# Expert weights read as one run of 16 or 8 KB per partition, with the tokens permuted to match

## The reference

```
p_group = softmax(h @ w_group);  g = argmax(p_group)
p_exp   = softmax((h @ w_expert) inside group g);  the best 2 experts, weights renormalised, times p_group[g]
for each expert e:   ffn[tokens of e] += weight * ((silu(h @ w_gate[e]) * (h @ w_up[e])) @ w_down[e])
h = layer_norm(ALPHA * h + ffn)
```

## Time and profile before

| | us |
|---|---|
| median of the timed runs | 2484.46 |
| the profiled execution, whole | 2484.86 |
| its span, first to last instruction | 2483.1 |
| TensorE busy | 2119.0 (85%) |
| VectorE busy | 667.5 |
| ScalarE busy | 313.5 |
| GpSimd busy | 175.2 |
| first and last gateup of layer 0 | 333.31 to 823.7 |
| first and last gateup of layer 1 | 1087.85 to 1576.4 |

### The profile page before, as it was taken

The page is one execution under the profiler, slowest core; times in us unless marked ns, Lnnn a source line. Parts: engine busy times, 40 slices in busy tenths (PEclk is TensorE's granted clock), DMA queues, the critical chain, the costliest instruction groups (busy, mean ns, idle before and its releaser), DMA issues. The chain is left out here.

```text
span 2483.1 us, 33384 instructions
## 1 busy us (share of the span) xinstructions
PE 2119.0 (85%) x13513; PEld 1427.3 (57%) x13513; DVE 667.5 (27%) x2009; ACT 313.5 (13%) x841; POOL 175.2 (7%) x224
## 2 busy tenths in 40 slices
PE   8999789888877498679878888488889989889997
PEld 7776466556555344366555555244478734448863
DVE  4354321111111315421111111328432112833211
ACT  2122000000000013100000000012322101222100
POOL 0112101000000100000000000100001100000110
PEclk9999867777888697767777777689899999989999
DMA  9333459999999742259999999852144342212420
GB/s 335 125 129 109 128 210 396 395 394 395 394 392 393 288 159 95 85 208 363 395 395 395 395 395 394 302 201 102 38 145 142 142 169 103 101 68 102 169 85 25
DMA packets 246122, 574.69 MB, mean 231 GB/s; under 512 B 13316, under 2 KB 16634, under 8 KB 245534
## 3 DMA queue, kind: packets, MB, share of 16 engines
q1 hardware_dynamic: 242974, 569.46, 62.0%
q0 software_dynamic: 3072, 4.21, 0.5%
HBM read 568.39 MB, written 9.44 MB: 233 GB/s over the span
## 5 line engine op out<-in xcount | busy, mean ns | idle before, releaser
L981 PE MATMUL ps<-ring,arena 128*32 128x256 f32 x3968 | 301.8, 469 | 107.6 <-DMA ring<-in_moe_w_up_dram 55.9
L981 PEld LDWEIGHTS ps<-ring,arena 128*32 128x32 f32 x3968 | 169.9, 135 | 250.5 <-issue 207.6
L2097 PE MATMUL ps<-arena,ring 128*128 128x256 f32 x1408 | 304.4, 379 | 1.6 <-DVE arena L244 1.6
L2097 PEld LDWEIGHTS ps<-arena,ring 128*128 128x128 f32 x1408 | 267.4, 190 | 38.5 <-DVE arena L244 2.3
L959 PEld LDWEIGHTS ps<-arena,h 128*128 128x128 f32 x2112 | 256.4, 202 | 29.5 <-issue 26.4
L959 PE MATMUL ps<-arena,h 128*128 128x32 f32 x2112 | 264.0, 286 | 3.0 <-DVE arena L949 3.0
L1394 PE MATMUL ps<-ring,arena 128*128 128x512 f32 (+1 forms) x576 | 250.9, 595 | 2.4 <-DVE arena L244 1.6
L1021 PE MATMUL ps<-ring,arena 128*32 128x256 f32 x1984 | 212.0, 602 | 38.1 <-issue 37.0
L266 PE MATMUL ps<-ring,arena 128*128 128x512 f32 x544 | 239.0, 602 | 1.6 <-DVE arena L1434 0.8
L1394 PEld LDWEIGHTS ps<-ring,arena 128*128 128x128 f32 x576 | 110.1, 193 | 136.2 <-issue 132.4
L266 PEld LDWEIGHTS ps<-ring,arena 128*128 128x128 f32 x544 | 104.8, 193 | 133.2 <-issue 130.4
(11 more groups left out here) (295 smaller groups left out, 1781.5 us busy)
## 6 DMA issues: line engine op xcount, KB each, us to landing
ring<-in_moe_w_gate_dram SPq DMA_DIRECT2D x62, 2048.0 KB, 19.4
ring<-in_moe_w_up_dram SPq DMA_DIRECT2D x62, 2048.0 KB, 22.4
ring<-in_moe_w_down_dram SPq DMA_DIRECT2D x62, 2048.0 KB, 19.8
ring<-in_w_up_dram SPq DMA_DIRECT2D x22, 2048.0 KB, 7.8
ring<-in_ssm_w_in_dram SPq DMA_DIRECT2D x12, 2048.0 KB, 12.2
ring<-in_w_in_dram SPq DMA_DIRECT2D x10, 2048.0 KB, 11.7
ring<-in_w_down_dram SPq DMA_DIRECT2D x10, 2048.0 KB, 7.8
ring<-in_attn_w_qkv_dram SPq DMA_DIRECT2D x6, 2048.0 KB, 20.2
```

The source lines that it names most:

```text
L981: mm = nc.tensor.matmul(ps[j * CAP:(j + 1) * CAP, 2 + b, 0:256], xg[:, b, k * CAP:(k + 1) * CAP], w[:, k, (j % 2) * 256:(j % 2 + 1) * 256] ...
L2097: mm = nc.tensor.matmul(ps[:, n % 4, 0:SEQ], w[:, k, k4 * P:(k4 + 1) * P], xT_mlp[:, k, :], start=(k == 0), stop=(k == KD - 1))
```

## The change

Gate and up matrices are read with `"(p k) n -> p k n"`: partition p gets the rows 8p to 8p + 7, which lie behind each other, 16 KB in all. Down matrices are read with `"(a p k) n -> p a k n"`, a = 2: partition p gets the rows 2p and 2p + 1 of each half of the matrix, two runs of 8 KB. Bytes, slots, the order of the loads and their waits stay. To match the new order of the contraction, pick takes its stationary operand from `h_rows`, a copy of h with the columns in the order k, p, that ScalarE makes once per layer in the place of `xT`; TensorE waits for it ahead of the first pick. And turn reads every second column of the hidden values.

```
         def dst(self, c, shape):
+            if len(shape) == 4:
+                return self.rows4(c).rearrange("p (a k) n -> p a k n", a=2)
...
-                add(cols8(t["moe_w_gate"][layer, e], 0, FF))
-                add(cols8(t["moe_w_up"][layer, e], 0, FF))
-                add(rows4(t["moe_w_down"][layer, e], 0))
+                add(t["moe_w_gate"][layer, e].rearrange("(p k) n -> p k n", p=P))
+                add(t["moe_w_up"][layer, e].rearrange("(p k) n -> p k n", p=P))
+                add(t["moe_w_down"][layer, e].rearrange("(a p k) n -> p a k n", a=2, p=P))
...
+            h_rows = area(0, TT, KD, P)
...
-                        nc.tensor.matmul(ps[:, b, k * CAP:(k + 1) * CAP], h[:, tt, k * P:(k + 1) * P],
+                        nc.tensor.matmul(ps[:, b, k * CAP:(k + 1) * CAP], h_rows[:, tt, k, :],
...
-                    mm = nc.tensor.matmul(ps[:, 4 + b, c2 * 64:(c2 + 1) * 64], hid[64:128, b, c2 * P:(c2 + 1) * P],
+                    mm = nc.tensor.matmul(ps[:, 4 + b, c2 * 64:(c2 + 1) * 64], hid[64:128, b, c2:256:2],
...
                             if part == 2:
-                                src, dst = w.rearrange("a (k p) n -> p (a k) n", p=P), ring.rows4(c)
+                                src = w.rearrange("e (a p k) n -> p (e a) k n", a=2, p=P)
+                                dst = ring.rows4(c).rearrange("p (a k) n -> p a k n", a=2)
                             else:
-                                src, dst = w.rearrange("a (k p) n -> p (a k) n", p=P), ring.rows8(c)
+                                src, dst = w.rearrange("e (p k) n -> p (e k) n", p=P), ring.rows8(c)
...
+                    pe.wait_ge(h_arranged.sem, h_arranged.at(1))
                     step_pick(pe, m, lambda s: s.at(1), None, 0, 0)
...
+                    act.wait_ge(route_pe.sem, route_pe.at(1))
+                    for tt in range(TT):
+                        ins = nc.scalar.activation(h_rows[:, tt, :, :], h[:, tt, :].rearrange("p (n k) -> p k n", k=KD),
+                                                   ACT.Copy)
+                    ins.then_inc(h_arranged.sem, 1)
```

More of the change, by code:

```diff
@@ L904, in hybrid_stack @@
         w1_loaded = sem("w1_loaded")
+        h_arranged = sem("h_arranged")
         NECOL = NE + 2
@@ L1087, in _ @@
                     for part, name in enumerate(("moe_w_gate", "moe_w_up", "moe_w_down")):
-                        sp.dma_start(w1[part], t[name][layer, 1].rearrange("(k p) n -> p k n", p=P))\
-                            .then_inc(w1_loaded.sem, 16)
+                        w = t[name][layer, 1]
+                        if part == 2:
+                            src = w.rearrange("(a p k) n -> p a k n", a=2, p=P)
+                            dst = w1[part].rearrange("p (a k) n -> p a k n", a=2)
+                        else:
+                            src, dst = w.rearrange("(p k) n -> p k n", p=P), w1[part]
+                        sp.dma_start(dst, src).then_inc(w1_loaded.sem, 16)
                     def load(e, half, used):
@@ L1122, in _ @@
                                 for part, name in enumerate(("moe_w_gate", "moe_w_up", "moe_w_down")):
-                                    w = t[name][layer, bass.ds(e, 1)].rearrange("a (k p) n -> p (a k) n", p=P)
-                                    dst = ring.rows4(first + part) if part == 2 else ring.rows8(first + part)
-                                    sp.dma_start(dst, w).then_inc(o["loaded"].sem, 16)
+                                    w = t[name][layer, bass.ds(e, 1)]
+                                    if part == 2:
+                                        src = w.rearrange("e (a p k) n -> p (e a) k n", a=2, p=P)
+                                        dst = ring.rows4(first + part).rearrange("p (a k) n -> p a k n", a=2)
+                                    else:
+                                        src, dst = w.rearrange("e (p k) n -> p (e k) n", p=P), ring.rows8(first + part)
+                                    sp.dma_start(dst, src).then_inc(o["loaded"].sem, 16)
                         sp.wait_ge(y_st[0].sem, 16 * (NE // 2) + 16 * (SEQ // CAP - 1) * NE)
@@ L1368, in moe @@
             turn_done()
-            for s, n in ((route_pe, 2), (route_act, 4), (route_dve, 5), (router_loaded, 32), (w1_loaded, 48), (pairs_loaded, 32)):
+            for s, n in ((route_pe, 2), (route_act, 4), (route_dve, 5), (router_loaded, 32), (w1_loaded, 48), (pairs_loaded, 32),
+                         (h_arranged, 1)):
                 s.advance(n)
```

## The result

The changed kernel takes 2424.03 us (2420.78 to 2426.21, four runs) against 2484.69 for the kernel before in the same measurement: ratio 0.9755, 95% interval 0.9738 to 0.9772. Predicted were 2420 and a range of 2404 to 2444. Measured once more beside other kernels it took 2421.38 us (ratio 0.9746, 0.9732 to 0.9760). By the medians the gain is 60.7 us, and 63.3 us in the second measurement. The profiled executions are 2484.86 and 2420.78 us long, 64.1 apart, where the sum of the prediction was 64.8; the profiled execution of the changed kernel is the shortest of its four.

The account below looks back on a forecast made before the run. The prediction took the weight loads to bound the expert stage; longer runs save 64.8 us over both layers, copy and strided columns 0, so 2484.9 - 64.8 = 2420.1, predicted as 2420 us, range 2404 to 2444.

Parts of the forecast that it names:

- What bounds the stage: Expert stage: weight loads set the time, 16.22 us per expert against 13.49 that TensorE needs.
- The price of a packet: Weight loads: a packet costs some 5 to 13 ns beside its bytes; longer runs give 15.06 us per expert, 1.16 less.
- the 0.39 us: Expert loads: the part of 16.22 us beyond the packet sum of 15.83, for scattered rows and semaphores, which stays.
- lower bound of the gain: Weight loads: nothing gained past 4 KB (420.5 GB/s for all), 0.87 us less per expert, 48.7 in all, so 2436.
- How much reaches the end: Load queue from expert 4 on: no gap comes back, so 32.4 us gained per layer, 64.8 in both.
- The copy and the strided operand: ScalarE's copy of h before the first pick, and turn's strided columns: each taken as 0.
- the two multiples: Copy's two activations: at twice 1.24 us each, 5.0 us, nothing late; at four times, 9.9, TensorE 3.8 late per layer.
- double cost: Turn's strided stationary loads at twice 207 ns: 0.8 us per expert, inside TensorE's slack of 1.6 from expert 9 on.
- (a): Weight loads: descriptors still cut at 2 and 4 KB, or memory sets the rate; time stays 2485; chance 0.06.
- (b): Expert stage: TensorE becomes the bound at a lower clock, mean 15.6 us per expert, gain 33, so 2452; chance 0.07.
- (c): Gate and up loads: 16 KB runs go slowly, at 0.75 us per packet 17.3 us per expert, so 2545; chance 0.04.

Follow-up runs that it names:

- halfdown: Changed kernel with half of each down matrix not loaded for experts 3 to 31; 2351.52 us, ratio 0.9458.
- r4k: Changed kernel with gate and up in four runs of 4 KB per partition, token copy permuted to match; 2445.93 us, ratio 0.9850.
- oldloads: Changed kernel's computing with the weight loads of the kernel before; 2485.11 us, ratio 1.0007.
- split2k: Changed kernel with gate and up interleaved in SBUF, so that their packets end after 2 KB, DRAM order unchanged; 2475.97 us, ratio 0.9962.
- r8k: Changed kernel with gate and up in two runs of 8 KB per partition, token copy permuted to match; 2429.64 us, ratio 0.9785.
- copy5: Changed kernel with three more strided activations on ScalarE ahead of the two that arrange the tokens; 2428.01 us, ratio 0.9764.
- experiment 3: Changed kernel with down matrices in 4 KB runs (2428.28 us) or 16 KB runs (2415.54); its table fits seven kernels' steps by 14.74 + n x 9.27 ns.
- down16: Changed kernel with down matrices in one 16 KB run per partition and turn as eight small matmuls; 2415.54 us, ratio 0.9721.

## Why the prediction was right

**What bounds the stage.** Right. The rate at which the queue moves packets set the step before and still does; halfdown moves the bound to TensorE only by taking bytes away.

**The price of a packet.** The mechanism was right, and the whole nearly: 15.06 us forecast, 15.02 measured, so a step got shorter by 1.20 us instead of 1.16. The parts were less good. From stretches of 3 to 13 us I had 13.5 ns beside the bytes between 2 and 4 KB and 5 between 4 and 8; it is 9.3 ns at every length. The table's line, less the 0.39 us that the prediction left for scattered rows and semaphores (no run measures that rest by itself), gives 84 ns for 2 KB, 159 for 4 KB, 308 for 8 KB and 607 for 16 KB; I had 84.7, 155.9, 307 and 610. The 4 KB price is the mis-sized one, and in the sum it hardly shows, since only 32 of the 160 packets are of 4 KB. It showed in r4k, where it stands for all of gate and up: 12 us wrong. The prediction's lower bound of the gain, nothing gained past 4 KB, is refuted by the same table.

**How much reaches the end.** Right: no gap came back. The weights are last from expert 10 on (9 forecast), and expert 31 starts at 786.77 (787 forecast). The gain to the last gateup is 66.9 us for 64.8, and 2.8 us of it are gone by the end: behind the start of expert 31 in layer 1 the kernel takes 913.1 us instead of 910.3. oldloads takes 911.6 for that part, split2k 911.4, r8k 913.3; of all fourteen traces the one of the kernel before is the shortest here. It is code that the change doesn't touch, and I have no cause for it. The two errors have opposite signs, so that 64.1 came so near to 64.8 is partly luck.

**The copy and the strided operand.** Nothing on the path, as taken. One strided activation takes 2.02 to 2.07 us and the two of them 3.98, against 1.24 for the dense one (which is another function, Identity with a scale and a bias, so the ratio isn't the stride's alone); that lies between the two multiples that I had worked out, and 2.3 us of room are left. That a late copy delays the whole stage was right too (copy5). The strided stationary loads of turn take 216 ns on average from 470 to 740 us, against 207 for the dense ones: no double cost. Issues did get shorter, from up to 10 us to 0.4 (experiment 3).

**The rivals.** (a) fell with the packet count, (b) with halfdown, (c) with a 16 KB packet at 607 ns, under the 682 where it would have decided. The rows called up for (b) were read wrongly: 462.25 is the start of expert 9, not 8, and of the 16.51 us of expert 7 TensorE was busy for 14.03 only and waited for 1.74 at its end. So no row showed TensorE itself needing over 16 us.

The forecast is 4.0 us under the first median and 1.4 under the second; two measurements of this kernel differ by 2.7 us.

**What a packet costs beside its bytes.** It is 9.3 ns of its engine, the same for 2, 4, 8 and 16 KB (experiment 3). The Trainium skill, "DMA: Bandwidth & Descriptors", section "Why small descriptors are slow (HBM only)", has a fixed overhead of about 3 cycles per packet; at the 850 MHz that the page gives for the fabric that is an estimated 3.5 ns. The runs agree that the overhead is fixed per packet and doesn't grow with its size, but not with its amount. By the page's figure the change would have been worth an estimated 128 x 3.5 ns x 55, some 25 us, instead of 64.

## What to carry to other kernels

Where a stage's GB/s row is flat and its DMA row at 9, count the packets: in this kernel each costs 9.3 ns of its engine beside its bytes, 11% of a 2 KB packet and 1.5% of one of 16 KB. A contraction's order is free, so a matrix of 2 KB rows can be read in runs of whole partitions if the other operand gets the same permutation, and that permutation should be made once, in a place where its engine is idle. Then look for stretches in which the queue stands: closing the one at this stage's start was worth 15 us, a quarter of what the longer packets brought, once TensorE's loop was written out.

## What the runs showed of the hardware

- With the other cores idle this core moves 428 GB/s in the stage with 16 KB packets (down16), 426 with 8 KB ones among them, and 394 with 2 and 4 KB. The time for the same bytes grows by 9.3 ns with each packet, over packets of 2 to 16 KB, to 0.02 us in 15.
- Source and destination written as three or four dimensions are joined where both are contiguous: 115,051 packets. If only the destination is not contiguous, the packet ends there (split2k, 229,738).
- With a queue full of 2 and 4 KB packets the issue of one 2 MB load holds SyncE for up to 10.3 us (kernel before); with 8 and 16 KB packets it is 0.3 to 0.4 us (changed kernel).
- A copy with a strided read (step 32 bytes) costs ScalarE 2.0 us for 128x1024 float32; a dense activation of that shape took 1.24.
- A TensorE loop over six experts stood for 9.5 us at each turn but the first in one of its two copies, with eight or nine code packets per turn there; the copy without waits had eight in its first turn and none after. Written out, the same work had none of these waits.
